# A mixer and expert kernel: the order ahead of the experts, and 368 dense tokens for 384

## The reference, cut to what matters

```python
sh1, sc1, g1, sh2, sc2, g2 = split(silu(c) @ w_ada + b_ada, 6)
z = modulate(rms_norm(x, norm1_g), sh1, sc1) @ w_in        # a, gate, u
hc = silu(layer_norm(causal_depthwise_conv(a * sigmoid(gate))))   # 31 taps
hs = s5(u)              # chunked state space, gelu, product with w_glu, sigmoid
x = x + g1 * (concat(hc, hs) @ w_out)
h2 = modulate(rms_norm(x, norm2_g), sh2, sc2)
q = h2 @ w_q            # 8 heads x 2 halves of 64; scores against 128 keys each
# top 16 of 128 by 128 pairs per head: 128 experts a token, of 16384
act = gelu(u_tab @ h2);  x = x + g2 * (gate * act) @ v_tab  # chosen experts only
y = modulate(rms_norm(x, final_norm_g), shift, scale)
```

## Time and profile before

| | us |
|---|---|
| median of 3 runs | 1853.5 (1851.95 to 1853.55) |
| profiled execution, its time | 1852.28 |
| its span, first to last instruction | 1850.4 |
| PE busy | 1760.4 (95%) |
| DVE busy | 1184.1 (64%) |
| ACT, POOL busy | 681.3 (37%), 689.1 (37%) |
| mean granted TensorE clock | 0.983 |
| ahead of the first product | 0 to 386.6 |
| first product | 386.6 to 1212.9 |
| second product | 1212.9 to 1829.2 |

### The profile page before, as it was taken

How to read it: one execution, slowest core, us unless ns; L and a number is a source line. 1 busy time by engine, 2 the same in 40 slices (tenths; PEclk the granted TensorE clock), 3 DMA queues, 4 the chain that set the end, 5 groups by cost and what they waited for, 6 DMA issues and landing times.

```text
span 1850.4 us, 33440 instructions
## 1 busy us (share of the span) xinstructions
PE 1760.4 (95%) x13287; PEld 1635.3 (88%) x13287; DVE 1184.1 (64%) x3089; ACT 681.3 (37%) x1212; POOL 689.1 (37%) x585
## 2 busy tenths in 40 slices
PE   5997888999999999999999999999999999999996
PEld 2984578799999999999999999988888888888895
DVE  8996944079994677777766760256666666666663
ACT  2331333233333444444444444333333333333333
POOL 1200012335446333333333334466555545555200
PEclk8999989999999999999999999999999999999998
DMA  8545422658888788888888787689988889888831
GB/s 289 137 75 204 158 85 69 228 142 241 243 239 242 221 240 249 246 249 256 258 242 252 243 246 244 240 297 364 341 318 316 316 316 336 327 317 315 297 127 46
DMA packets 305708, 442.72 MB, mean 239 GB/s; under 512 B 24753, under 2 KB 221537, under 8 KB 303505
## 3 DMA queue, kind: packets, MB, share of 16 engines
q1 hardware_dynamic: 280416, 366.35, 62.3%
q0 software_dynamic: 25136, 74.24, 11.2%
HBM read 377.37 MB, written 130.25 MB: 274 GB/s over the span
## 4 chain that ended last, share of the span: by engine, by line
PE 91%; DVE 3%; DMA 3%; ACT 2%; issue 1%; POOL 0%; DVEq 0%; SPq 0%; POOLq 0%; ACTq 0%
PE ps L1844 40%; PE ps L1872 28%; PE ps L1587 8%; PE ps L1833 5%; PE ps L1823 3%; DMA raw<-in_w_ada 2%; PE ps L1542 1%; PE ps L1559 1%; PE ps L1761 1%; DVE rstd L1057 1%; DMA v_rows_ring<-v_rows,v_row_index 1%; PE ps L1745 1%; PE ps L1620 1%; PE ps L1792 0%; PE ps L1666 0%
## 5 line engine op out<-in xcount | busy, mean ns | idle before, releaser
L1844 PE MATMUL ps<-h,hl 128*128 128x256 f32 (+1 forms) x6144 | 823.7, 288 | 1.4 <-DVE sc L1318 1.4
L1844 PEld LDWEIGHTS ps<-h,hl 128*128 128x128 f32 x6144 | 761.8, 189 | 1.6 <-DVE sc L1318 1.6
L823 ACT ACTIVATE hl<-raw 128x512 fp32r<-128x512 f32 x512 | 322.4, 630 | 720.3 <-PE ps L1844 475.9
L1872 PEld LDWEIGHTS ps<-WH,hl 128*128 128x128 f32 x3072 | 531.7, 188 | 30.3 <-issue 28.5
L1872 PE MATMUL ps<-WH,hl 128*128 128x384 f32 x3072 | 545.1, 338 | 1.3 <-ACT actr L856 1.3
L621 POOL TENSOR_TENSOR hl<-raw,hl 128x512 fp32r<-128x512 f32 x260 | 352.0, 1355 | 498.2 <-ACT hl L823 498.1
L1498 DVE TENSOR_TENSOR hl<-raw,hl 128x512 fp32r<-128x512 f32 x252 | 174.6, 693 | 232.1 <-ACT hl L823 232.0
L1427 DVE TENSOR_SCALAR ohA<-ps,selT 128x128 f32<-128x128 f32 x384 | 134.1, 349 | 146.2 <-PE ps L1833 133.5
L638 POOL DMA_INDIRECT v_rows_ring<-v_rows,v_row_index x136 | 129.1, 949 | 202.9 <-PE ps L1823 170.5
L629 POOL DMA_INDIRECT gathered_act<-act_spill,act_index x136 | 152.6, 1122 | 43.5 <-issue 41.3
L1428 DVE TENSOR_SCALAR ohB<-ps,selT 128x128 f32<-128x128 f32 x384 | 154.7, 403 | 0.0
(11 more groups left out here) (281 smaller groups left out, 1299.9 us busy)
## 6 DMA issues: line engine op xcount, KB each, us to landing
raw<-in_u SPq DMA_DIRECT2D x128, 512.0 KB, 6.4
v_rows<-in_v SPq DMA_DIRECT2D x128, 512.0 KB, 5.8
raw<-in_v SPq DMA_DIRECT2D x128, 512.0 KB, 5.3
act_spill<-actr SPq DMA_DIRECT2D x128, 260.0 KB, 2.9
raw<-in_w_ada SPq DMA_DIRECT2D x64, 512.0 KB, 4.6
gate_spill<-stage SPq DMA_DIRECT2D x24, 1024.0 KB, 7.5
hring<-act_spill SPq DMA_DIRECT2D x128, 192.0 KB, 4.0
gbp<-gate_spill SPq DMA_DIRECT2D x16, 1536.0 KB, 7.3
```

The costliest lines, as they stand in the source:

```text
L823: act.activation(hl[:, n % 2, 0, c], raw[:, n % NRAW, c], ACT.Copy).then_inc(s_whi, 1)
L1844: last = pe.matmul(ps[:, 2 * (m % 2) + h, 0:b - a], hl[:, m % 2, w, q * P:(q + 1) * P], h2[:, r, q, a:b], start=q == 0 and (w, r) == (0, 0 ...
L1872: last = pe.matmul(ps[:, mm % 2, 0:ND], hl[:, mm % 2, w, j * P:(j + 1) * P], WHL[b % 2][:, r, j, :], start=j == 0 and (w, r) == (0, 0), st ...
```

## The change

Two things are changed. Ahead of the experts the order of PE's, DVE's and ACT's lists and of the weight stream is another: rows of pairs 1 and 2 stand inside the `in` product, the preparation and the y stage, the PSUM banks of the y stage and the GLU product are others so that banks 6 and 7 stay free for them, `modulations(1)` stands behind S, the GLU weights are issued by POOL, the high copy of the convolution's rows is made by ACT. In the experts `ND` is 368 in place of 384, and 152 tokens are gathered in 38 groups of 4, one every 3 steps.

```diff
-TILES = ((0, 128), (128, 256), (256, 384), (384, 452), (452, 520))
+TILES = ((0, 128), (128, 256), (256, 368), (368, 444), (444, 520))
-GT = 68
+GT = 76
-          + ada(1, 0, KD) + tiles_of("out", 0, 1)
-          + ada(2, 0, KD) + tiles_of("out", 2, 3, 4, 5, 6, 7)
-          + tiles_of("q", 0, 1) + ada(3, 0, 2)
-          + [tile for f in range(2, KD) for tile in tiles_of("q", f) + ada(3, f, f + 1)])
+          + ada(1, 0, KD) + ada(2, 0, KD) + tiles_of("out", 0, 1, 2, 3, 4, 5, 6, 7)
+          + tiles_of("q", 0, 1) + ada(3, 0, 3)
+          + [tile for f in range(2, KD - 1) for tile in tiles_of("q", f) + ada(3, f + 1, f + 2)]
+          + tiles_of("q", KD - 1))
+        CHUNK_BANKS = ((0, 3), (1, 4), (2, 5), (0, 3))
+        GLU_BANKS = ((1, 2), (0, 3))
...
-            g = (mm - VR0) * 3 // 10
-            return g if mm >= VR0 and g < NGG and (mm == VR0 or (mm - 1 - VR0) * 3 // 10 != g) else None
+            g, rest = divmod(mm - VR0, 3)
+            return g if mm >= VR0 and g < NGG and rest == 0 else None
... SP
-                if n == FIRST["out"]:
-                    sp.wait_ge(s_cpj, 1)
-                    for w in range(CT):
-                        sp.dma_start(h1[:, CT + w, 0:CC], dr["w_glu"][w]).then_inc(s_gw, 16)
... POOL, behind the stores of conv_p and conv_s
+            pool.wait_ge(s_cpj, 1)
+            for w in range(CT):
+                pool.dma_start(h1[:, CT + w, 0:CC], dr["w_glu"][w]).then_inc(s_gw, 16)
... ACT
+            split_hi(FSP["in"], hlm)
             act.wait_ge(s_hs, 1)
...
-                if k == 0:
-                    split_hi(FSP["in"], hlm)
-                if k == 4:
+                if k == 6:
                     split_hi(FSP["in"] + 1, hlm)
...
-            split_hi(FSP["out"], hlm)
-            split_hi(FSP["out"] + 1, hlm)
             for t in range(CT):
                 act.wait_ge(s_glu, t + 1)
...
                 last.then_inc(s_gsig, 1)
+            split_hi(FSP["out"], hlm)
+            split_hi(FSP["out"] + 1, hlm)
...
+                act.wait_ge(s_hcm, t + 1)
+                act.activation(rhi[:, t, :], mixin[:, t, :], ACT.Copy).then_inc(s_rh, 1)
... DVE
-                if q == 1:
+                if q == 0:
                     split_lo(FSP["in"])
-                if q == 6:
+                if q == 7:
                     split_lo(FSP["in"] + 1)
...
-            modulations(1)
...
+            modulations(1)
             conv_taps(AFTER_SCAN, tuple(range(CT)))
-            split_lo(FSP["out"])
-            split_lo(FSP["out"] + 1)
             for t in range(CT):
...
-            conv_taps(5, tuple(range(CT)))
+            conv_taps(3, tuple(range(CT)))
+            split_lo(FSP["out"])
+            split_lo(FSP["out"] + 1)
             rows_lo(slice(CT, KD), 1)
...
-                dve.tensor_copy(rhi[:, t, :], mixin[:, t, :]).then_inc(s_rh, 1)
...
+            link(dve.memset(selv[96:P, TPD - 1, 2, :], 0.0))
... PE
-                        after(pe, s_mods, pair)
+                        after(pe, s_ade, pair)
...
-                if q % 4 == 3:
-                    modulation_rows(0, 2 + q // 4, 3 + q // 4)
-            modulation_rows(0, 4, KD)
+                if q % 2 == 1:
+                    modulation_rows(0, 2 + q // 2, 3 + q // 2)
+            modulation_rows(0, 6, KD)
...
+                if t >= 10:
+                    modulation_rows(1, t - 10, t - 9)
... in the convolution's matmuls (w), and in the preparation (e)
+                    if w == 16:
+                        modulation_rows(1, 5, 6)
...
-                    modulation_rows(1, 0, 2)
+                    modulation_rows(1, 4, 5)
...
+                if e in (4, 8, 14, 17):
+                    modulation_rows(1, PAIR_AT[e], PAIR_AT[e] + 1)
...
-            modulation_rows(1, 3, 5)
...
-            direct_chunks(0, 0, ST)
-            modulation_rows(1, 5, KD)
-            direct_chunks(1, 0, ST // 2)
+            direct_chunks(0, 0, 3 * ST // 4)
             pe.wait_ge(s_cve, 1)
             modulation_columns(1)
-            pe.wait_ge(s_mods, 2)
-            direct_chunks(1, ST // 2, ST)
+            modulation_rows(2, 0, 2)
+            direct_chunks(1, 0, 3 * ST // 4)
+            modulation_rows(2, 2, 3)
             pe.wait_ge(s_S, 1)
...
+                if t == 3 * ST // 4:
+                    pe.wait_ge(s_z, 1)
+                    direct_chunks(0, t, ST)
+                    direct_chunks(1, t, ST)
...
+            modulation_rows(2, 3, 5)
             pe.wait_ge(s_gw, 16 * CT)
-            pe.wait_ge(s_z, 2)
+            pe.wait_ge(s_z, 3)
...
-            modulation_rows(2, 0, KD - 1)
+            modulation_rows(2, 5, KD)
...
-            split_dense("q", hl, (h2[:, 0], h2[:, 1]), s_qe, s_q, lambda t: modulation_rows(3, t + 1 if t else 0, min(t + 2, KD)))
+            modulation_rows(3, 0, 3)
+            split_dense("q", hl, (h2[:, 0], h2[:, 1]), s_qe, s_q,
+                        lambda t: modulation_rows(3, t + 2, t + 3) if 0 < t < KD - 2 else None)
...
-            pe.wait_ge(s_scd, NTT)
+            pe.wait_ge(s_scd, NTT - 1)
```

More of the change, by code:

```diff
@@ L759, in chunk_outputs @@
                 act.activation(Ysb[:, b].rearrange("p i (g h q) -> p g h i q", h=2, q=SQ)[:, :, g2],
-                               ps[0:NC + TS, 4 * g2 + b, :].rearrange("p (g i q) -> p g i q", g=4, i=L),
+                               ps[0:NC + TS, CHUNK_BANKS[b][g2], :].rearrange("p (g i q) -> p g i q", g=4, i=L),
                                ACT.Copy).then_inc(s_Ye, 1)
@@ L766, in gelu_y @@
                     act.activation(yT[:, t, h * 256:(h + 1) * 256].rearrange("p (i c) -> p i c", i=4),
-                                   ps[:, 4 * h + t, 0:4 * (NC + TS)].rearrange("p (i c) -> p i c", i=4)[:, :, 0:NC],
+                                   ps[:, CHUNK_BANKS[t][h], 0:4 * (NC + TS)].rearrange("p (i c) -> p i c", i=4)[:, :, 0:NC],
                                    ACT.Gelu_apprx_tanh)
-                act.activation(yT[:, t, TP:T], ps[:, t, NC:NC + TS], ACT.Gelu_apprx_tanh).then_inc(s_z, 1)
+                act.activation(yT[:, t, TP:T], ps[:, CHUNK_BANKS[t][0], NC:NC + TS], ACT.Gelu_apprx_tanh).then_inc(s_z, 1)
             for t in range(CT):
@@ L781, in _ @@
                 for h, (a, b) in enumerate(HALVES):
-                    last = act.activation(uT[:, t, a:b], ps[:, 2 * (t % 2) + h, 0:b - a], ACT.Sigmoid)
+                    last = act.activation(uT[:, t, a:b], ps[:, GLU_BANKS[t % 2][h], 0:b - a], ACT.Sigmoid)
                 last.then_inc(s_gsig, 1)
+            split_hi(FSP["out"], hlm)
+            split_hi(FSP["out"] + 1, hlm)
             act.wait_ge(s_hsm, CT)
@@ L1267, in _ @@
                 if t:
-                    conv_split(t - 1)
-            conv_split(CT - 1)
+                    rows_lo(t - 1, t + 1)
+            rows_lo(CT - 1, CT + 1)
             a1 = [PW[:, a, :, 1:2].broadcast_to([P, ST, TS]) for a in (0, 1)]
@@ L1548, in modulation_columns @@
                 pe.wait_ge(s_ade, pair + 1)
+                after(pe, s_mods, pair)
                 for j in range(4):
@@ L1632, in _, with second_modulations @@
                 sum_squares("rms1", q)
-                if q % 4 == 3:
-                    modulation_rows(0, 2 + q // 4, 3 + q // 4)
-            modulation_rows(0, 4, KD)
+                if q % 2 == 1:
+                    modulation_rows(0, 2 + q // 2, 3 + q // 2)
+            modulation_rows(0, 6, KD)
             modulation_columns(0)
-            split_dense("in", hlm, (rhi, h1lo), None, s_win)
+            def second_modulations(t):
+                if t >= 10:
+                    modulation_rows(1, t - 10, t - 9)
+            split_dense("in", hlm, (rhi, h1lo), None, s_win, second_modulations)
             pe.wait_ge(s_Xr, 3)
@@ L1642, in _ @@
             X = (XR, XI)
+            PAIR_AT = {4: 2, 8: 3, 14: 6, 17: 7}
             def chunk_inputs():
@@ L1696, in _ @@
                 last.then_inc(s_prep, 1)
-                if e == 15:
-                    modulation_rows(1, 2, 3)
             pe.wait_ge(s_cpe, 4)
@@ L1708, in _ @@
             pe.wait_ge(s_prepe, 20)
-            modulation_rows(1, 3, 5)
             def chunk_out(t, g):
-                return ps[0:NC + TS, 4 * g + t // 4, (t % 4) * P:(t % 4 + 1) * P]
+                return ps[0:NC + TS, CHUNK_BANKS[t // 4][g], (t % 4) * P:(t % 4 + 1) * P]
             def direct_chunks(g, first, last_):
@@ L1737, in y_rows @@
                     c = (i % 4) * (NC + TS)
-                    last = pe.transpose(ps[:, 4 * (i // 4) + t, c:c + n], Ysb[0:n, t, i, :], ident[0:n, 0:n])
+                    last = pe.transpose(ps[:, CHUNK_BANKS[t][i // 4], c:c + n], Ysb[0:n, t, i, :], ident[0:n, 0:n])
                 last.then_inc(s_yt, 1)
             for t in range(ST):
+                if t == 3 * ST // 4:
+                    pe.wait_ge(s_z, 1)
+                    direct_chunks(0, t, ST)
+                    direct_chunks(1, t, ST)
                 for a in range(2):
@@ L1757, in _ @@
```

(10 more changed lines are left out.)

4 lines of the change are left out of this document (removed).

## The result

The changed kernel takes 1834.2 us (median of 4 runs, 1831.4 to 1836.0) where the kernel before takes 1853.5 (1852.0 to 1854.0, 4 runs). The ratio is 0.9896, with an interval of 0.9881 to 0.9912. It is 19 us faster where 32 were forecast, and its median lies 0.2 us outside the upper end of the range. The profiled execution took 1833.53 us with a span of 1831.7; before it was 1852.28 and 1850.4.

What follows compares the result with a forecast made beforehand. Both expert products were taken as bound by the number and length of their matmuls, with moves paying only ahead of 386.6 us. Gains of 11.0 + 3.5 + 8.9 + 8.0 = 31.4 us gave 1821.5 us, range 1811 to 1834.

Steps and rivals of the forecast that it cites:

- Second product: Second expert product, 384 to 368 columns: -20.9 us for columns, +8.4 for gathered groups, +1.5 for the start, net -11.0 us.
- Rival (d): Second product: weight load is the limit and columns do not count, 20.9 us do not come, 1842 us; chance 0.04.
- The smaller slope that the prediction weighed as a rival: Second product: 0.13 ns a column from the skill's issue gaps, saving 6.4 us, so the part would lose; no separate chance.
- Rival (c): Second product: the DMA engines give out, 1850 us, slower than before below 322 GB/s; chance 0.07, of it slower 0.02.
- 0.426 ns a column: Second product: matmul cost per column between 260 and 384; sixteen columns off 3072 matmuls gain 20.9 us.
- Up to the mean: Ahead of the experts, up to the convolution's mean: new order makes the mean at 229.3 for 237.85 us; part sums to -8.9.
- Rival (a): Ahead of the mean: the vector engine's idle time does not come, 7.6 us gained too, 1814 us; chance 0.15.
- keeps some 4 to 5 us of waits for copies and one tile: TensorE between 121.9 us and the y stage: waits that remain, giving 51 us and a y stage start at 173.
- rival (b): Front gives half: rows wait for `w_ada` tiles through a ring of four, the 8.9 us are gone, 1830 us; chance 0.17.
- It stands idle 7.6 us: Vector engine after 24 taps, from 184.7 us: waits for the first sigmoid until 192.3 us.
- two are left, 2.9: Column sums ahead of the mean: tiles 3 and 0 summed earlier, two behind the last tap take 2.9 us, formerly 5.66.
- Queries: Query products: second tile's product at 327.7 to 329.4 us (5.7 gained), 1.0 for rows, 1.3 for a score copy; -8.0 us.

Runs made afterwards that it cites:

- 40 taps: Changed kernel with AFTER_SCAN 40 for 24, so 16 more convolution taps run ahead of the first sigmoid: 1820.1 us, ratio 0.9815.
- the stores moved: Kernel before with only the four convolution-state stores moved behind the first chunk outputs: 1852.4 us, ratio 0.9994.
- the widths: Kernel before with the second product's matmul width varied by block (256 to 384 columns), output incomplete; ran once, only distances read, no time given.
- the better version: Changed kernel with state stores moved, AFTER_SCAN 40 and WH rows 384 apart: 1811.6 us; with 352 dense tokens and 42 groups on top: 1796.5 us.
- the experts' part alone: Kernel before with only ND 368, 38 gathered groups, one every 3 steps, and the memset; old order ahead: 1842.2 us, ratio 0.9942.
- the order alone: Changed kernel with ND 384 and 34 groups as before, only the order ahead of the experts new: 1846.4 us, ratio 0.9961.
- the stride: Changed kernel with WH0 and WH1 rows laid out 384 apart (1536 bytes) and 368 columns used: 1832.7 us, one time.

## Why the prediction was right, and where it failed

**What bounds** was right: both products follow the number and length of their matmuls, and ahead of them the moved instructions paid where they stood on the path.

**First product**: -3.5 us forecast, 827.6 to 824.0 measured. Right.

**Second product**: -11.0 forecast, -7.9 measured. Rival (d), that the columns don't count, is out: one stair is 6.7 ns. The smaller slope that the prediction weighed as a rival, by which the cut would have saved 6.4 us, is out as well: the lines give 15.6. Rival (c), that the DMA engines give out, is out too: 344 GB/s at a share of 0.93 from 1240 to 1500 us, and no group behind the third waits. The term that was mis-sized is "0.426 ns a column": -20.9 forecast, -15.6 in the lines' busy times. The slope itself was good (0.42 by the stairs). What the step left out is that `WH` also gets rows of 368 values, and that costs 3.8 us by the busy times with and without it; with rows 384 apart the cut gives 19.4 of the 20.9. The groups cost 7.7 us for 8.4, and the start 0.5 for 1.5: group 1 was not the one that waited 0.7 us more, group 0 waited 1.83 and group 2 0.38, where before 1.7 us were waited in all. These two give 1.7 us back.

**Modulation rows of pair 0**: no gain forecast, `mods` at 42.9 us for 43.1. Right.

**Up to the mean**: -8.9 forecast, +0.6 measured by the end of the second norm's sums. Rival (a), that the vector engine's idle time does not come, is out: it came. Here the prediction failed, in these steps:

- "keeps some 4 to 5 us of waits for copies and one tile. That is 51 us from 121.9, so 173." The y stage began at 178.7. The one tile took 16.6 us to land for the 5.4 of the earlier trace rows, since it was now issued while the stores' small pieces filled the DMA engines. The earlier trace rows had the sign in it: a share of 0.50 at 94 GB/s from 122 to 151 us. It was read as room for tiles, and the stretch's parts were not looked at. The working also asked what the change moves past the POOL queue, and not what stands in that queue at the time to which the tiles are moved. This was rival (b)'s outcome (its 8.9 us are gone) by a cause that (b) did not have: it reckoned with the ring of four places. That the time lies only 0.2 us outside the range is no merit of the sum: the range reached to 1834 because it took in (b). Moved away, the stores give the GLU product its 188 us, the mean is at 231.6 for 229.3, and the time falls by 5.6 us.
- "It stands idle 7.6 us." Right in kind: it was 10.7 (by the late product). But it was only booked as a loss, and the first thing to ask was what could fill it. Sixteen taps that stood behind the last split give 14 us, more than the part's whole forecast.
- "The rows that hid nothing at 211 to 233 us [...] now end at about 209." They ended at 215.4 us, and the tiles of `out` behind them in the ring landed at 216.6 (6.6 us after their issue at 210.0), so the splits came at 216.4: 0.8 us of waiting on the vector engine.
- "two are left, 2.9", and the sums behind the mean, which were not priced: both ran at the low clock. TensorE now stands idle 14.37 us ahead of the last column sums, and the clock over 211 to 233 us is 0.64 (it was 0.91), over 232 to 240 us 0.50, that is 1.2 GHz throughout. The eight last column sums take 3.83 us (with 40 taps all sixteen take 3.77, with no rest ahead of them), so the mean waits 4.00 us and not 2.9. The squares' sums that follow take about 6.1 us for the 3.9 of before. These are 1.1 and 2.2 us on the path. With 40 taps the column sums no longer wait, but the sums of the squares, behind 6.0 us of idle time, still take 5.7:

```profile
240.96 3.89 PE L1620 MATMUL ps<-sq,ones 128*128 128x256 f32 x16 [2.23 <-ACT sq L686]
```
```profile
224.66 5.71 PE L1619 MATMUL ps<-sq,ones 128*128 128x256 f32 x16 [6.04 <-ACT sq L688]
```

  In all eight traces with the new order these sums take 5.3 to 6.3 us, whatever the rest ahead of them (3.2 to 6.0 us); in the four with the old order they take 3.9 us twice and 5.5 twice (the stores moved, and the widths), behind the same 2.2 us of rest. So the loss stays in the better version, but it does not grow with the rest just ahead, and only part of it belongs to the new order.

Part of the difference is also the one execution on which the sum rests. Three more kernels have the order of before (the experts' part alone, the stores moved, the widths), and they made the mean at 234.6, 233.9 and 233.8 us, not at 237.9. Two more have the order of after (the order alone, the stride), and they made it at 234.6 and 238.9, beside 236.5. So by these traces the new order does not make the mean sooner at all. The first product is apart in all of them: at 385.1 to 386.6 us with the old order, at 376.9 to 381.9 with the new. A scatter of 3 to 4 us between executions bounds how well a front of this kind can be read from one trace, and the microseconds of the list above are those of one execution.

**Queries**: -8.0 forecast, -7.8 measured; the second tile's product at 329.7, just behind the forecast's 327.7 to 329.4, and held by its split as said. Right, though the rows at 312.2 waited 2.65 us for a tile and ended as the first q product began, at 315.3 (314.5 before).

So of 12.7 missing microseconds the stores explain 5.6, by the time with them moved (the GLU product was 5.4 us late), and the low clock at the sums 3.3. In the second product the pitch gave 5.3 less, of it 3.8 by the operand's layout, and the groups, the start and the rest of the product 2.1 more than forecast. What remains, about half a microsecond, is of the size of the splits' wait for `out`, which no run isolated.

## What to carry to other kernels

Before a load is moved to a quiet stretch, look at the DMA share and the GB/s of that stretch in pieces of a few microseconds: a high share at low GB/s means that small pieces are draining there, and a load will wait behind them. When an engine is freed from one wait, look for its next one, and move work that stands behind that wait ahead of it; the forecast had the idle time in it and did not use it. And price an operand's width and its layout apart: cut columns in the steps in which the measured pitch falls, and keep the rows as far apart as they were until another distance has been measured.
